# A two-layer hybrid model on one core: dense layer rows without their scale, and a last addition by column halves

## The chip, the cores and the metric

The kernel runs on one core of a Trainium2 chip. A time is that of one execution on the device in microseconds (us); what is shown for a kernel is the median of its runs. The core has TensorE (PE, with its weight loads apart as PEld), VectorE (DVE), ScalarE (ACT), GpSimd (POOL) and SyncE (SP, which here only starts transfers). They run side by side and wait for each other by semaphores: an instruction adds one to a semaphore when it is done, and another waits until the semaphore has reached a value.

## The reference

256 tokens of width 1024 go through two layers. The first is windowed attention and a dense gated layer, the second a gated delta rule and eight experts of which each token takes two. The stretches in which the change lies are the end of attention, the start of the dense layer, and the end of the experts:

```python
def rms_norm(x, w):
    y = x * rsqrt(mean(x * x, axis=-1, keepdims=True) + EPS)
    return y * w
def swiglu(h, w_gate, w_up, w_down):
    return (silu(h @ w_gate) * (h @ w_up)) @ w_down

h = h + swa_sink_attention(rms_norm(h, a_norm), ...)
h = h + swiglu(rms_norm(h, f_norm), f_w_gate, f_w_up, f_w_down)      # D_FF = 3584
h = h + gated_deltanet(rms_norm(h, b_norm), ...)
h = h + moe_swiglu(rms_norm(h, m_norm), ...)                          # 8 experts, top 2
return rms_norm(h, final_norm)
```

## The kernel before, in words

Tokens lie in two tiles of 128 rows (`t` = 0, 1) and 1024 columns; `h` holds the sum that runs through the layers. All products are in float32, made of three products each: the weights and the activations are split into a high part (ACT copies it, rounded) and a low part (DVE subtracts), and `mm3` (lines 342 to 345) adds high by high, low by high and high by low. Weights come from memory in pieces of 1 MB (`n`), through six raw buffers (`w_raw`), and are split into three buffers (`w_high`, `w_low`). `split_high` (line 331) waits until the piece has landed and until TensorE has used the piece three before it (`w_used`), and `split_low` (line 335) waits for `split_high`; SP starts the transfer of a piece when the piece six before it has been split (`lo_done`).

Every engine has one program, written out by hand; within it instructions run in the order in which they stand. So what the change does depends on which instruction stands where.

**From attention to the dense layer.** The output product of attention is made in pieces `out_piece(half, t, cb, bank)`; a piece is 12 products of 512 columns. The last four are those of `half` 1: t=0 with column blocks 0 and 1, then t=1 with 0 and 1. DVE adds each to `h` (`added`, line 2107). When a row tile of `h` is complete, ACT squares and sums it (`norm_tile`, line 693), POOL makes the reciprocal root (`norm`, lines 462 and 463: `rstd`), and DVE multiplies the rows by `rstd` and by the gain `f_gain` (`norm_tile`, line 2213: `xs`). TensorE turns these rows by eight transposes (`turn_tile`, line 1258), ACT and DVE make the high and the low part of the turned rows (lines 699 and 2115: `x_high`, `x_low`), and TensorE multiplies the first gate block with them (`first_gate(half, t)`, four pieces of 12 products). Then `up` and, in a loop over seven blocks of 512 columns, gate, up and down products follow. ACT applies silu (line 802), DVE multiplies the up product with it (`gated`, line 2286).

**The end of the experts.** Seven experts give their rows back through memory; POOL gathers them, and DVE adds them to `h` (line 2798). The rows of the eighth expert go back by products with a selection matrix (`last_back(b)`, lines 1974 and 1977, one for each half `b` of the 1024 columns; its result for t and b lies in bank 4 + 2t + b), and DVE adds them (`last_add(t, b)`, line 2745). Between the two stands the job loop, a loop over jobs 8 to 10 on each engine: it runs its body only where an expert has more than 128 tokens, and with these inputs there is no such job (the trace has 336 expert weight pieces, which are 8 experts of 42). Each engine reads the number of jobs into a register (`value_load`) and goes through the loop, three times over the body. Then ACT squares and sums the rows of `h` (line 676), POOL makes `rstd` (lines 462 and 463), DVE multiplies (`fin`, line 2843), and SP stores the four quarters.

Semaphore `added` counts the additions to `h` at the end; `last_ps` counts the last products.

Of the kernel before, what the change touches and what calls it, by code (L numbers as in the profile page):

```python
# [12 lines left out]
D = 1024  # L13
T = 256
TT = T // 128
KD = D // 128
F = 3584
CH = 512
# [67 lines left out]
def hybrid_kernel(nc, x, a_w_qkv, a_b_qkv, a_sinks, a_w_o, f_w_gate, f_w_up, f_w_down,  # L86
# [13 lines left out]
    with ExitStack() as ctx:  # L100
# [20 lines left out]
        col_w = sb("col_w", [128, NCOL])  # L121
        ss = sb("ss", [128, 5, TT])
        ms = sb("ms", [128, 5, TT])
        rstd = sb("rstd", [128, 5, TT])
# [321 lines left out]
        def _(pool):  # L446
# [181 lines left out]
            for st in ("att", "ffn", "gdn", "moe"):  # L628
# [19 lines left out]
                deltanet_pool()  # L648
            norm("fin")


        @block.scalar
        def _(act):
# [48 lines left out]
            def attention(n0):  # L702
# [22 lines left out]
                def probs_out(a):  # L725
                    t = ITEMS[a][1]
                    act.wait_ge(sem("probT_ps"), a + 1)
                    if a >= 2:
# [3 lines left out]
                        .then_inc(sem("probT_done"), 1)  # L732

                def o_high(half, t):
                    act.wait_ge(sem("tile_ps"), 2 * half + t + 1)
                    nc.scalar.activation(xH[:, 4 * half:4 * half + 4, 128 * t:128 * t + 128],
                                         PS[:, 0, :].rearrange("p (k c) -> p k c", k=4), ACT.Copy).then_inc(sem("tile_high"), 1)
# [51 lines left out]
                o_high(1, 1)  # L789
                norm_tile("ffn", 0)  # L790
                split_high(act, f0 + 1)
                turn_tile("ffn", 0)
                norm_tile("ffn", 1)
                split_high(act, f0 + 2)
                turn_tile("ffn", 1)
                split_high(act, f0 + 3)

            def ffn(n0):
                def silu(n, r):
                    act.wait_ge(w_used, n + r * RAW)  # L800
                    for t in range(TT):
                        nc.scalar.activation(fg[:, t], PS[:, t, :], ACT.Silu).then_inc(sem("f_silu_done"), 1)

                def turned(c):
                    for t in range(TT):
                        act.wait_ge(sem("f_turn_ps"), 2 * c + t + 1)
                        nc.scalar.activation(faH[:, t], PS[:, 6 + t, :].rearrange("p (f q) -> p f q", f=4), ACT.Copy)\
                            .then_inc(sem("f_high_done"), 1)

                silu(n0 + 2, 0)  # L810
                act.wait_ge(xs_done, TT * (norm_no["ffn"] + 1))
# [279 lines left out]
            def experts(n0):  # L1091
# [95 lines left out]
                with act.Fori(E, JOBS) as j:  # L1187
                    with act.If(j < njobs):
                        r0 = j * NC
                        turned_in(j)  # L1190
                        for n in range(4):
                            split_high(act, n0 + n, r0)
                        silu(n0 + 2, r0)
                        split_high(act, n0 + 4, r0)
                        split_high(act, n0 + 5, r0)
                        with act.Fori(0, NC - 1) as i:
                            step(r0 + i)
                        turned(r0 + NC - 1)
                        y_high(n0 + SUBS_FFN, r0)

            if "att" in stages:
# [5 lines left out]
            if "moe" in stages:  # L1207
                experts(base["moe"])
            norm("fin")


        @block.tensor
        def _(pe):
# [47 lines left out]
            def attention(n0):  # L1261
# [149 lines left out]
                out_piece(1, 0, 1, 3)  # L1411
                out_piece(1, 1, 0, 4)
                out_piece(1, 1, 1, 5)

            def ffn(n0):
# [11 lines left out]
                x0 = TT * norm_no["ffn"]  # L1427
                turn_tile("ffn", xs, 0, xs_done, x0 + 1)
                first_gate(0, 0)
                first_gate(1, 0)  # L1430
                turn_tile("ffn", xs, 1, xs_done, x0 + 2)
                first_gate(0, 1)
# [449 lines left out]
            def experts(n0):  # L1882
# [86 lines left out]
                def last_back(b):  # L1969
                    o = [PS[:, 4 + 2 * t + b, :] for t in range(TT)]  # L1970
                    c = slice(CH * b, CH * b + CH)
                    pe.wait_ge(sem("ys_high"), b + 1)
                    for t in range(TT):
# [5 lines left out]
                def back(j):  # L1979

                    pe.wait_ge(sem("ys_low"), j + 3)
                    for t in range(TT):
                        for b in range(2):
                            o = PS[:, 4 + 2 * t + b, :]
# [50 lines left out]
                pe.wait_ge(sem("m_act_done"), E * NC)  # L2035
                turned()
                pe.wait_ge(sem("m_low_done"), E * NC)
                last_down(n0 + 4, E * NC - 1)

                pe.wait_ge(sem("jobs_done"), 1)  # L2040
                njobs = pe.value_load(jobs[0:1, NJ:NJ + 1], min_val=E, max_val=JOBS)
                with pe.Fori(E, JOBS) as j:
                    with pe.If(j < njobs):
                        r0 = j * NC
                        pe.wait_ge(sem("ys_low"), 2)
                        pe.wait_ge(sem("added"), 4 * j)
                        turn_in(j)
# [11 lines left out]
                        back(j - E)  # L2059
                pe.wait_ge(sem("added"), njobs * 4)  # L2060
                last_back(0)
                last_back(1)

# [11 lines left out]
        def _(dve):  # L2075
# [42 lines left out]
            def attention(n0):  # L2118
# [162 lines left out]
            def ffn(n0):  # L2281
                def gated(c, n, r):
                    dve.wait_ge(w_used, n + r * RAW)
                    for t in range(TT):
                        dve.wait_ge(sem("f_silu_done"), 2 * c + t + 1)
                        V.tensor_tensor(fa[:, t], PS[:, 2 + t, :], fg[:, t], ALU.mult).then_inc(sem("f_act_done"), 1)

# [13 lines left out]

                dve.sem_inc(sem("f_y_free"), 1)
                gated(0, n0 + 4, 0)
                split_low(dve, n0 + 5)
# [16 lines left out]
            def deltanet(n0):  # L2321
                def last_gated(t):
                    return V.tensor_tensor(fa[:, t], PS[:, 2 + t, :], fg[:, t], ALU.mult)

# [306 lines left out]
            def experts(n0):  # L2631
# [92 lines left out]
                def add(c, e):  # L2724
                    dve.wait_ge(sem("back_ps"), c + 1)
                    dve.wait_ge(sem("added"), 4 * (LAST + 1) + 4 * c)
                    for t in range(TT):
                        for b in range(2):
                            col = slice(CH * b, CH * b + CH)
# [71 lines left out]
                last_y_low(0)  # L2801
                last_y_low(1)
                with dve.Fori(E, JOBS) as j:
                    with dve.If(j < njobs):
# [14 lines left out]
                        add(j - E, e)  # L2819
                dve.wait_ge(sem("added"), njobs * 4)  # L2820
                for t in range(TT):
                    for b in range(2):
# [60 lines left out]
```

## Time and profile before

| what | us |
|---|---|
| median of 3 runs | 1541.15 |
| lowest and highest run | 1535.83, 1541.67 |
| the profiled execution's own time | 1540.96 |
| its span | 1539.2 |
| PE busy | 1502.5 (98%) |
| DVE busy | 1211.9 (79%) |
| ACT busy | 974.6 (63%) |
| POOL busy | 148.8 (10%) |

The span is the time from the first to the last instruction that the profiler recorded; the execution's own time is 1.76 us longer. A row of the timeline gives start, duration, engine, line, operation, what is written and read, and in brackets how long the engine had been idle before, and which instruction ended that. A matmul of 512 columns is shown as 0.39 us, but the next one starts 0.23 us after it, since they are pipelined.

### The profile page before, as it was taken

To read this page: it belongs to the slowest core of one execution; us is meant where nothing else is said; L and a number is where in the kernel's file an instruction comes from. 1 tells how busy PE (TensorE), PEld (TensorE's weight loads), DVE (VectorE), ACT (ScalarE), POOL (GpSimd) and SP (SyncE) were. 2 spreads that over 40 slices of the span, in tenths; PEclk is the share of its full clock that TensorE was granted. 3 is DMA by queue.
4 is the path that set the end of the run, shared out by engine and by line. 5 is a ranking of instruction groups with operands and counts; after the bars stand their busy time and mean duration, and the time that the engine had idled before them with its cause. 6 is when DMAs were issued, how large, how long until landed. Compare 5 with 4: busy or idle time off the path is not lost.

```text
span 1539.2 us, 22172 instructions
## 1 busy us (share of the span) xinstructions
PE 1502.5 (98%) x8236; PEld 1260.7 (82%) x8236; DVE 1211.9 (79%) x947; ACT 974.6 (63%) x789; POOL 148.8 (10%) x159
## 2 busy tenths in 40 slices
PE   7999999999999999999999999999999999999996
PEld 6878888879997888888888888888888888888885
DVE  6764555556785568888888888888889888888987
ACT  5544333345555347777777777777777777777774
POOL 1021000001424109300000000000000000000100
PEclk9999999999999999999999999999999999999999
DMA  9349555555331228999999999999999999999992
GB/s 365 109 153 401 196 186 184 191 163 167 110 109 57 81 85 325 403 415 392 372 366 403 374 369 392 375 379 381 378 379 379 379 377 379 392 368 365 423 399 102
DMA packets 90971, 455.05 MB, mean 296 GB/s; under 512 B 7712, under 2 KB 8112, under 8 KB 47920
## 3 DMA queue, kind: packets, MB, share of 16 engines
q1 hardware_dynamic: 83984, 430.86, 73.7%
q0 software_dynamic: 6080, 22.29, 3.7%
q10 hardware_dynamic: 864, 1.29, 0.3%
q8 instruction: 32, 0.52, 0.1%
q14 instruction: 11, 0.09, 0.0%
HBM read 438.68 MB, written 15.73 MB: 295 GB/s over the span
## 4 chain that ended last, share of the span: by engine, by line
PE 92%; DVE 3%; ACT 2%; POOL 1%; issue 1%; DMA 0%; DVEq 0%; SPq 0%; POOLq 0%; ACTq 0%
PE PS L343 28%; PE PS L345 27%; PE PS L344 27%; PE PS L1576 2%; PE PS L1941 2%; PE PS L1330 1%; DVE w_low L335 1%; PE PS L1556 1%; PE PS L1304 0%; DMA w_raw<-in_a_w_qkv 0%; PE PS L1992 0%; ACT w_high L331 0%; PE PS L1319 0%; PE PS L1453 0%; DVE cv L2366 0%
## 5 line engine op out<-in xcount | busy, mean ns | idle before, releaser
L335 DVE TENSOR_TENSOR w_low<-w_raw,w_high 128x2048 fp32r<-128x2048 f32 x406 | 931.4, 2297 | 177.6 <-ACT w_high L331 176.8
L331 ACT ACTIVATE w_high<-w_raw 128x2048 fp32r<-128x2048 f32 x406 | 777.5, 1918 | 287.1 <-PE PS L345 282.1
L343 PE MATMUL PS<-w_high,x_high 128*128 128x512 f32 x1264 | 502.7, 398 | 5.2 <-DVE x_low L2115 2.1
L345 PE MATMUL PS<-w_high,x_low 128*128 128x512 f32 x1264 | 494.1, 391 | 0.0
L344 PE MATMUL PS<-w_low,x_high 128*128 128x512 f32 x1264 | 493.2, 390 | 0.0
L343 PEld LDWEIGHTS PS<-w_high,x_high 128*128 128x128 f32 x1264 | 238.2, 188 | 56.4 <-DVE w_low L335 4.0
L345 PEld LDWEIGHTS PS<-w_high,x_low 128*128 128x128 f32 x1264 | 237.7, 188 | 51.0
L344 PEld LDWEIGHTS PS<-w_low,x_high 128*128 128x128 f32 x1264 | 238.3, 189 | 46.9
L343 PE MATMUL PS<-w_high,m_act_high 128*128 128x512 f32 x448 | 175.1, 391 | 1.6 <-DVE m_act_low L2760 1.6
L344 PE MATMUL PS<-w_low,m_act_high 128*128 128x512 f32 x448 | 174.4, 389 | 0.0
L345 PE MATMUL PS<-w_high,m_act_low 128*128 128x512 f32 x448 | 174.4, 389 | 0.0
L343 PEld LDWEIGHTS PS<-w_high,m_act_high 128*128 128x128 f32 x448 | 84.1, 188 | 19.0 <-DVE m_act_low L2760 1.8
L345 PEld LDWEIGHTS PS<-w_high,m_act_low 128*128 128x128 f32 x448 | 84.1, 188 | 17.5
L344 PEld LDWEIGHTS PS<-w_low,m_act_high 128*128 128x128 f32 x448 | 84.1, 188 | 17.3
L1137 ACT ACTIVATE m_act_high<-PS 128x512 fp32r<-128x512 f32 x56 | 33.5, 599 | 70.1 <-PE PS L1941 70.1
L343 PE MATMUL PS<-x_high,w_high 128*128 128x256 f32 x192 | 56.1, 292 | 0.0
L344 PE MATMUL PS<-x_low,w_high 128*128 128x256 f32 x192 | 54.3, 283 | 0.0
L345 PE MATMUL PS<-x_high,w_low 128*128 128x256 f32 x192 | 54.3, 283 | 0.0
L524 POOL DMA_DIRECT2D x_slots<-x_slots_dram x6 | 3.2, 534 | 502.5 <-PE PS L1992 502.5
L2756 DVE TENSOR_TENSOR m_act<-PS,m_gate 128x512 f32<-128x512 f32 x56 | 38.3, 684 | 1.2 <-PE PS L345 1.2
L2760 DVE TENSOR_TENSOR m_act_low<-PS,m_act_high 128x512 fp32r<-128x512 f32 x56 | 38.2, 683 | 0.0
L343 PE MATMUL PS<-w_high,f_act_high 128*128 128x512 f32 x96 | 37.6, 391 | 0.0
(324 smaller groups left out, 1231.3 us busy)
## 6 DMA issues: line engine op xcount, KB each, us to landing
w_raw<-in_m_w_blocks SPq DMA_DIRECT2D x336, 1024.0 KB, 7.1
w_raw<-in_b_w_in SPq DMA_DIRECT2D x16, 1024.0 KB, 5.4
w_raw<-in_f_w_gate SPq DMA_DIRECT2D x14, 1024.0 KB, 5.0
w_raw<-in_f_w_up SPq DMA_DIRECT2D x14, 1024.0 KB, 5.1
w_raw<-in_f_w_down SPq DMA_DIRECT2D x14, 1024.0 KB, 4.8
x_slots_dram<-zeros POOLq DMA_DIRECT2D x12, 512.0 KB, 8.2
w_raw<-in_a_w_qkv SPq DMA_DIRECT2D x5, 1024.0 KB, 17.3
w_raw<-in_a_w_o SPq DMA_DIRECT2D x4, 1024.0 KB, 15.4
```

Of the source, the lines that this page charges most:

```text
L331: nc.scalar.activation(WH[:, n % SPLIT, :], W[:, n % RAW, :], ACT.Copy).then_inc(hi_done, 1)
L335: nc.vector.tensor_tensor(WL[:, n % SPLIT, :], W[:, n % RAW, :], WH[:, n % SPLIT, :].bitcast(f32), ALU.subtract).then_inc(lo_done, 1)
L343: nc.tensor.matmul(o, sH, mH, start=first, stop=False)
L344: nc.tensor.matmul(o, sH, mL, start=False, stop=False)
L345: return nc.tensor.matmul(o, sL, mH, start=False, stop=last)
L1137: nc.scalar.activation(maH[:], PS[:, 4, :].rearrange("p (f q) -> p f q", f=4), ACT.Copy)\
L1330: last = nc.tensor.matmul(PS[:, 1, (AD + 1) * hh:(AD + 1) * (hh + 1)], probT[:, a % 2, hh * (t + 1) + kt, :], vals[:, kt, g, :], start=(kt ...
L1556: last = nc.tensor.matmul(PS[:, bank + hg, 128 * (hh % 4):128 * (hh % 4) + 128], lhs(hh), rhs(hh), start=True, stop=True)
L1576: last = nc.tensor.matmul(PS[halves(s), INV + s, HALF * hh:HALF * hh + HALF], lhs(s, hh), rhs(s, hh), start=True, stop=True)
L1941: last = nc.tensor.transpose(PS[:, 4, 128 * f:128 * f + 128], ma[:, 128 * f:128 * f + 128], ident)
L2756: V.tensor_tensor(ma[:], PS[:, 1, :], mg[:], ALU.mult).then_inc(sem("m_act_done"), 1)
L2760: V.tensor_tensor(maL[:], PS[:, 4, :].rearrange("p (f q) -> p f q", f=4), maH[:].bitcast(f32), ALU.subtract).then_inc(sem("m_low_done"), 1)
```

## The change

Two parts. In the dense layer the rows go to TensorE as `h` times the gain, without `rstd`; the scale is applied behind the products instead, inside silu (`scale=rstd`) and inside the multiplication with the up product. The order of the instructions at the entry of the dense layer changes with it on DVE, ACT and TensorE, and the squares are written to `prob` instead of `xs`. At the end, TensorE's `last_back` and DVE's `last_add` come ahead of the job loop, additions go by column halves, ACT squares each half of 512 columns after the job loop, and POOL adds the two half sums in the `tensor_scalar` that it has anyway. TensorE reads the number of jobs ahead of its last down products.

```diff
+            n = norm_no["fin"]
+            for t in range(TT):
+                s = slice(t, t + 1)
+                pool.wait_ge(ss_done, TT * n + t + 1)
+                link(nc.gpsimd.tensor_scalar(ss_half[:, 0, s], ss_half[:, 0, s], 1.0 / D, EPS, ALU.mult, ALU.add))
+            for t in range(TT):
+                s = slice(t, t + 1)
+                pool.wait_ge(ss_done, TT * n + TT + t + 1)
+                link(nc.gpsimd.tensor_scalar(ms[:, n, s], ss_half[:, 1, s], 1.0 / D, ss_half[:, 0, s], ALU.mult, ALU.add))
+                nc.gpsimd.tensor_tensor(rstd[:, n, s], ms[:, n, s], neg_half[:, s], ALU.pow).then_inc(rstd_done, 1)
...
+                def dense_square(t):
+                    n = norm_no["ffn"]
+                    act.wait_ge(h_done, TT * (n - 1) + t + 1)
+                    nc.scalar.activation(prob[:, t], h[:, t].rearrange("p (n k) -> p n k", n=AG), ACT.Square, accum_out=ss[:, n, t:t + 1]).then_inc(ss_done, 1)
...
-                norm_tile("ffn", 0)
+                turn_tile("ffn", 0)
                 split_high(act, f0 + 1)
-                turn_tile("ffn", 0)
-                norm_tile("ffn", 1)
+                dense_square(0)
+                turn_tile("ffn", 1)
                 split_high(act, f0 + 2)
-                turn_tile("ffn", 1)
+                dense_square(1)
                 split_high(act, f0 + 3)
...
-                        nc.scalar.activation(fg[:, t], PS[:, t, :], ACT.Silu).then_inc(sem("f_silu_done"), 1)
+                        nc.scalar.activation(fg[:, t], PS[:, t, :], ACT.Silu, scale=rstd[:, norm_no["ffn"], t:t + 1]).then_inc(sem("f_silu_done"), 1)
...
+                for b in range(2):
+                    c = slice(CH * b, CH * b + CH)
+                    for t in range(TT):
+                        act.wait_ge(sem("added"), njobs * 4 + (TT * b + t + 1))
+                        nc.scalar.activation(xs[:, t, c], h[:, t, c], ACT.Square, accum_out=ss_half[:, b, t:t + 1]).then_inc(ss_done, 1)
...
                 out_piece(1, 1, 0, 4)
+                turn_tile("ffn", xs, 0, xs_done, TT * norm_no["ffn"] + 1)
                 out_piece(1, 1, 1, 5)
...
-                turn_tile("ffn", xs, 0, xs_done, x0 + 1)
                 first_gate(0, 0)
+                turn_tile("ffn", xs, 1, xs_done, x0 + 2)
                 first_gate(1, 0)
-                turn_tile("ffn", xs, 1, xs_done, x0 + 2)
...
                 turned()
+                pe.wait_ge(sem("jobs_done"), 1)
+                njobs = pe.value_load(jobs[0:1, NJ:NJ + 1], min_val=E, max_val=JOBS)
                 pe.wait_ge(sem("m_low_done"), E * NC)
                 last_down(n0 + 4, E * NC - 1)
-
-                pe.wait_ge(sem("jobs_done"), 1)
-                njobs = pe.value_load(jobs[0:1, NJ:NJ + 1], min_val=E, max_val=JOBS)
+                last_back(0)
+                last_back(1)
                 with pe.Fori(E, JOBS) as j:
...
-                pe.wait_ge(sem("added"), njobs * 4)
-                last_back(0)
-                last_back(1)
...
-                    dve.wait_ge(rstd_done, TT * n + t + 1)
-                    dve.wait_ge(h_done, t + 1)
-                    V.scalar_tensor_tensor(out=xs[:, t], in0=h[:, t], scalar=rstd[:, n, t:t + 1], in1=f_gain[:],
-                                           op0=ALU.mult, op1=ALU.mult).then_inc(xs_done, 1)
+                    dve.wait_ge(h_done, TT * (n - 1) + t + 1)
+                    V.tensor_tensor(xs[:, t], h[:, t], f_gain[:], ALU.mult).then_inc(xs_done, 1)
...
+                norm_tile(0)
                 added(1, 1, 0)
-                norm_tile(0)
+                turn_tile("ffn", 0)
                 added(1, 1, 1)
-                turn_tile("ffn", 0)
+                norm_tile(1)
                 split_low(dve, f0 + 1)
-                norm_tile(1)
                 turn_tile("ffn", 1)
...
-                        V.tensor_tensor(fa[:, t], PS[:, 2 + t, :], fg[:, t], ALU.mult).then_inc(sem("f_act_done"), 1)
+                        V.scalar_tensor_tensor(out=fa[:, t], in0=PS[:, 2 + t, :], scalar=rstd[:, norm_no["ffn"], t:t + 1], in1=fg[:, t],
+                                               op0=ALU.mult, op1=ALU.mult).then_inc(sem("f_act_done"), 1)
...
+                dve.wait_ge(sem("added"), 4 * E)
+                for b in range(2):
+                    for t in range(TT):
+                        dve.wait_ge(sem("last_ps"), 2 * b + t + 2)
+                        last_add(t, b).then_inc(sem("added"), 1)
                 with dve.Fori(E, JOBS) as j:
...
-                dve.wait_ge(sem("added"), njobs * 4)
-                for t in range(TT):
-                    for b in range(2):
-                        dve.wait_ge(sem("last_ps"), 2 * b + t + 2)
-                        last = last_add(t, b)
-                    last.then_inc(h_done, 1)
```

How the instructions stand. On TensorE, at the entry of the dense layer, before; `x_high` is the turned row tile, `xs` the rows that are turned, and each row with a wait is the first of 12 products, of which the others are left out:

```order
L343 MATMUL PS<-w_high,x_high 128x512 [waits tile_low,lo_done]
...
L1258 MATMUL PS<-cst,xs 128x128 [waits xs_done]
L1258 MATMUL PS<-cst,xs 128x128 x7
L343 MATMUL PS<-w_high,x_high 128x512 [waits tile_low,lo_done]
...
L343 MATMUL PS<-w_high,x_high 128x512 [waits tile_low,lo_done]
...
L1258 MATMUL PS<-cst,xs 128x128 [waits xs_done]
L1258 MATMUL PS<-cst,xs 128x128 x7
L343 MATMUL PS<-w_high,x_high 128x512 [waits tile_low,lo_done]
```

and in the changed program, from the output piece ahead of the last one (line 1278 is the transposes' line there):

```order
L344 MATMUL PS<-w_high,x_high 128x512 [waits tile_low,lo_done]
...
L1278 MATMUL PS<-cst,xs 128x128 [waits xs_done]
L1278 MATMUL PS<-cst,xs 128x128 x7
L344 MATMUL PS<-w_high,x_high 128x512 [waits tile_low,lo_done]
...
L344 MATMUL PS<-w_high,x_high 128x512 [waits tile_low,lo_done]
...
L1278 MATMUL PS<-cst,xs 128x128 [waits xs_done]
L1278 MATMUL PS<-cst,xs 128x128 x7
L344 MATMUL PS<-w_high,x_high 128x512 [waits tile_low,lo_done]
```

Before, tile 0 is turned behind the last output piece and tile 1 behind both gate pieces of tile 0; now tile 0 is turned ahead of the last output piece and tile 1 between the two gate pieces of tile 0.

On DVE at the same place, before (line 2107 adds to `h`, 2213 scales the rows, 2115 is the low part of the turned rows, 335 that of the weights):

```order
L2107 TENSOR_TENSOR h<-PS,h 128x512 [waits piece_ps]
L2107 TENSOR_TENSOR h<-PS,h 128x512 [waits w_used]
L2213 SCALAR_TENSOR_TENSOR xs<-h,rstd,f_gain 128x1024 [waits h_done,rstd_done,loaded_att]
L2107 TENSOR_TENSOR h<-PS,h 128x512 [waits w_used]
L2115 TENSOR_TENSOR x_low<-PS,x_high 128x4x128 [waits tile_high] x2
L335 TENSOR_TENSOR w_low<-w_raw,w_high 128x2048 [waits hi_done]
L2213 SCALAR_TENSOR_TENSOR xs<-h,rstd,f_gain 128x1024 [waits h_done,rstd_done,loaded_att]
L2115 TENSOR_TENSOR x_low<-PS,x_high 128x4x128 [waits tile_high] x2
```

and now:

```order
L2125 TENSOR_TENSOR h<-PS,h 128x512 [waits piece_ps]
L2230 TENSOR_TENSOR xs<-h,f_gain 128x1024 [waits h_done,loaded_att]
L2125 TENSOR_TENSOR h<-PS,h 128x512 [waits w_used]
L2133 TENSOR_TENSOR x_low<-PS,x_high 128x4x128 [waits tile_high] x2
L2125 TENSOR_TENSOR h<-PS,h 128x512 [waits w_used]
L2230 TENSOR_TENSOR xs<-h,f_gain 128x1024 [waits h_done,loaded_att]
L336 TENSOR_TENSOR w_low<-w_raw,w_high 128x2048 [waits hi_done]
L2133 TENSOR_TENSOR x_low<-PS,x_high 128x4x128 [waits tile_high] x2
```

The rows of tile 1 (`xs`) now stand ahead of the low part of the weight piece, and both stand behind the last addition to `h`.

On TensorE at the end, before, from the last of the down products to the loop, and then from the loop's end:

```order
L345 MATMUL PS<-w_high,m_act_low 128x512
L2041 TENSOR_LOAD jobs [waits jobs_done]
L2041 ISA x2
L2042 UNCONDITIONAL_BRANCH
L2043 COMPARE_AND_BRANCH
...
L2042 COMPARE_AND_BRANCH
L2060 REGISTER_ALU
L1974 MATMUL PS<-y_last_high,pick_last 128x512 [waits ys_high,added]
```

and now:

```order
L346 MATMUL PS<-w_high,m_act_low 128x512
L1995 MATMUL PS<-y_last_high,pick_last 128x512 [waits ys_high,added]
L1995 MATMUL PS<-y_last_high,pick_last 128x512
L1998 MATMUL PS<-y_last_low,pick_last 128x512 [waits ys_low]
L1998 MATMUL PS<-y_last_low,pick_last 128x512
L1995 MATMUL PS<-y_last_high,pick_last 128x512 [waits ys_high,added]
L1995 MATMUL PS<-y_last_high,pick_last 128x512
L1998 MATMUL PS<-y_last_low,pick_last 128x512 [waits ys_low]
L1998 MATMUL PS<-y_last_low,pick_last 128x512
L2064 UNCONDITIONAL_BRANCH
```

The register load and the loop no longer stand between the last down product and the products that bring the rows back. The loop's body is 262 rows on TensorE; on DVE it is 55 and on ACT 41, and there it now stands between the additions and `fin`, and still ahead of the squares.

## Rows read from the trace of the kernel before

**Rows 1.** The page, part 1.
```profile
PE 1502.5 (98%) x8236; PEld 1260.7 (82%) x8236; DVE 1211.9 (79%) x947; ACT 974.6 (63%) x789; POOL 148.8 (10%) x159
```

**Rows 2.** Waits of PE: total us, times, longest.
```profile
PE PS L1974 <- issue: 2.4, 1, 2.4
PE PS L343 <- DVE x_low L2115: 2.1, 2, 1.1
```

**Rows 3.** PE's timeline, dense entry: start, duration, engine, line, what, idle before.
```profile
99.42 0.39 PE L343 MATMUL PS<-w_high,x_high 128*128 128x512 f32 x1
...
104.25 0.47 PE L343 MATMUL PS<-w_high,x_high 128*128 128x512 f32 x1 [1.07 <-DVE x_low L2115]
...
109.84 1.04 PE L1258 MATMUL PS<-cst,xs 128*128 128x128 f32 x8
111.94 0.47 PE L343 MATMUL PS<-w_high,x_high 128*128 128x512 f32 x1 [1.06 <-DVE x_low L2115]
...
117.47 0.39 PE L343 MATMUL PS<-w_high,x_high 128*128 128x512 f32 x1
```

**Rows 4.** PE's timeline, dense loop: eight transposes with no wait behind them.
```profile
139.24 1.03 PE L1453 MATMUL PS<-cst,f_act 128*128 128x128 f32 x8
140.03 0.48 PE L343 MATMUL PS<-w_high,x_high 128*128 128x512 f32 x1
```

**Rows 5.** DVE's timeline, dense entry.
```profile
100.23 1.27 DVE L2213 SCALAR_TENSOR_TENSOR xs<-h,rstd,f_gain 128x1024 f32<-128x1024 f32 x1
102.34 0.69 DVE L2107 TENSOR_TENSOR h<-PS,h 128x512 f32<-128x512 f32 x1 [0.84 <-PE PS L345]
...
104.61 2.28 DVE L335 TENSOR_TENSOR w_low<-w_raw,w_high 128x2048 fp32r<-128x2048 f32 x1
```

**Rows 6.** ACT's timeline, dense entry.
```profile
99.68 1.92 ACT L331 ACTIVATE w_high<-w_raw 128x2048 fp32r<-128x2048 f32 x1 [0.90 <-PE PS L345]
```

**Rows 7.** DVE's groups in the dense layer: count, busy us, mean ns, idle before.
```profile
L2286 DVE TENSOR_TENSOR f_act<-PS,f_gate 128x512 f32<-128x512 f32 x12 | 7.7, 682 | 5.1 <-PE PS L345 5.1
```

**Rows 8.** Stretches of the dense layer and of the experts: PE, PEld, DVE, ACT, POOL.
```profile
128.00:340.00 212.00, 212.00 (x965) 176.00 (x964) 117.64 (x88) 85.80 (x66) 2.95 (x6) 1.00 0.62 213
1000.00:1200.00 200.00, 200.00 (x912) 165.27 (x911) 177.40 (x99) 149.33 (x101) 2.14 (x4) 1.00 0.98 381
```

**Rows 9.** DMA issues: count, KB each, median us to landing.
```profile
w_raw<-in_m_w_blocks SPq DMA_DIRECT2D x336, 1024.0 KB, 7.1
```

**Rows 10.** PE's timeline, end.
```profile
1520.44 0.50 PE L343 MATMUL PS<-w_high,m_act_high 128*128 128x512 f32 x1 [1.59 <-DVE m_act_low L2760]
...
1525.79 0.39 PE L345 MATMUL PS<-w_high,m_act_low 128*128 128x512 f32 x1
1528.58 0.70 PE L1974 MATMUL PS<-y_last_high,pick_last 128*128 128x512 f32 x2 [2.40 <-issue]
```

**Rows 11.** DVE's timeline, end.
```profile
1526.85 0.69 DVE L2741 TENSOR_TENSOR y_last_low<-PS,y_last_high 128x512 fp32r<-128x512 f32 x1 [0.67 <-ACT y_last_high L1146]
1529.62 2.92 DVE L2745 SCALAR_TENSOR_TENSOR h<-PS,cw,h 128x512 f32<-128x512 f32 x4 [2.08 <-PE PS L1977]
1533.48 1.41 DVE L2843 SCALAR_TENSOR_TENSOR fin<-h,rstd,w_fin 128x512 f32<-128x512 f32 x2 [0.94 <-POOL rstd L463]
1535.34 1.41 DVE L2843 SCALAR_TENSOR_TENSOR fin<-h,rstd,w_fin 128x512 f32<-128x512 f32 x2 [0.45 <-POOL rstd L463]
```

**Rows 12.** The chain that ended last: start, us, what.
```profile
1530.47 2.08 DVE h L2745 x3
```

**Rows 13.** ACT's timeline, end.
```profile
1526.22 0.60 ACT L1146 ACTIVATE y_last_high<-PS 128x512 fp32r<-128x512 f32 x1 [0.76 <-PE PS L345]
...
1532.57 1.06 ACT L676 ACTIVATE xs<-h 128x1024 f32<-128x1024 f32 x1 [0.17 <-DVE h L2745]
```

**Rows 14.** POOL's timeline, end.
```profile
1532.50 0.19 POOL L462 TENSOR_SCALAR ms<-ss 128x1 f32<-128x1 f32 x1 [95.03 <-ACT xs L676]
...
1533.81 0.48 POOL L462 TENSOR_SCALAR ms<-ss 128x1 f32<-128x1 f32 x1 [0.46 <-ACT xs L676]
```

More of the change, by code:

```diff
@@ L122, in hybrid_kernel @@
         ss = sb("ss", [128, 5, TT])
+        ss_half = sb("ss_half", [128, 2, TT])
         ms = sb("ms", [128, 5, TT])
@@ L648, in _ @@
                 deltanet_pool()
-            norm("fin")
+            n = norm_no["fin"]
[8 more added lines that the diff above has]
+                nc.gpsimd.tensor_tensor(rstd[:, n, s], ms[:, n, s], neg_half[:, s], ALU.pow).then_inc(rstd_done, 1)
         @block.scalar
@@ L808, in turned @@
                             .then_inc(sem("f_high_done"), 1)
+                act.wait_ge(rstd_done, TT * (norm_no["ffn"] + 1))
                 silu(n0 + 2, 0)
@@ L1208, in _ @@
                 experts(base["moe"])
-            norm("fin")
         @block.tensor
@@ L1971, in last_back @@
                     c = slice(CH * b, CH * b + CH)
+                    pe.wait_ge(sem("added"), 1)
                     pe.wait_ge(sem("ys_high"), b + 1)
@@ L2044, in experts @@
                         r0 = j * NC
-                        pe.wait_ge(sem("ys_low"), 2)
-                        pe.wait_ge(sem("added"), 4 * j)
+                        pe.wait_ge(sem("added"), 4 * j + 4)
                         turn_in(j)
@@ L2302, in ffn @@
                 dve.sem_inc(sem("f_y_free"), 1)
+                dve.wait_ge(rstd_done, TT * (norm_no["ffn"] + 1))
                 gated(0, n0 + 4, 0)
@@ L2322, in last_gated @@
                 def last_gated(t):
-                    return V.tensor_tensor(fa[:, t], PS[:, 2 + t, :], fg[:, t], ALU.mult)
+                    return V.scalar_tensor_tensor(out=fa[:, t], in0=PS[:, 2 + t, :], scalar=rstd[:, norm_no["ffn"], t:t + 1], in1=fg[:, t],
+                                                  op0=ALU.mult, op1=ALU.mult)
                 def last_low_turned(t):
@@ L2725, in add @@
                     dve.wait_ge(sem("back_ps"), c + 1)
-                    dve.wait_ge(sem("added"), 4 * (LAST + 1) + 4 * c)
-                    for t in range(TT):
-                        for b in range(2):
+                    dve.wait_ge(sem("added"), 4 * (E + 1) + 4 * c)
+                    for b in range(2):
+                        for t in range(TT):
                             col = slice(CH * b, CH * b + CH)
@@ L2802, in experts @@
                 last_y_low(1)
+                dve.wait_ge(sem("added"), 4 * E)
+                for b in range(2):
+                    for t in range(TT):
+                        dve.wait_ge(sem("last_ps"), 2 * b + t + 2)
+                        last_add(t, b).then_inc(sem("added"), 1)
                 with dve.Fori(E, JOBS) as j:
@@ L2819, in experts @@
                         add(j - E, e)
-                dve.wait_ge(sem("added"), njobs * 4)
-                for t in range(TT):
-                    for b in range(2):
-                        dve.wait_ge(sem("last_ps"), 2 * b + t + 2)
-                        last = last_add(t, b)
-                    last.then_inc(h_done, 1)
             if "att" in stages:
```

## The prediction

> **What bounds the kernel now.** I read the page first. TensorE is busy for 98% of the span and no other engine for more than 79% [rows 1], so what counts is where TensorE waits, and the chain behind its last product. The waits of TensorE come second. Apart from the start of the program, where it waits for the first weights, the two longest groups are 2.4 us of "issue" ahead of the products of line 1974, and twice 1.1 us for `x_low` of line 2115 [rows 2]. The change works at exactly these two places. Third, the timelines of the two stretches, for the sum. Fourth, the rest: in the dense loop and in the experts TensorE is busy for the whole of its stretch [rows 8], so a microsecond won at the entry of the dense layer should arrive at the end, as long as the weights keep up.
>
> **Part 1, the entry of the dense layer.** Before, TensorE starts the last output piece at 99.42 and the first `up` product at 117.47 [rows 3]: 18.05 us for five pieces and two turns of a tile. Each turn costs eight transposes and a wait until the turned rows are split; from the transposes' start at 109.84 to the next product at 111.94 it is 2.10 us. Where TensorE doesn't wait behind eight transposes, they take 0.79 us (139.24 to 140.03 [rows 4]), and the next product 0.08 us more than the others.
>
> The new path, from the same 99.42: the rows of tile 0 are made as soon as `h` of tile 0 is complete, some 1.3 us [rows 5] (its last piece is issued one piece, 2.72 us, ahead of 99.42, and its addition starts some 0.4 us after that and takes 0.7: 97.6), so they are there at 98.9 and the transposes start at once, to 100.21. The last output piece takes 12 steps of 0.227 us and 0.08: TensorE issues its last product at 102.79 and is free at 103.0. The first gate piece needs `x_low` of tile 0, which was finished under the output piece, and ends at 105.75. Its cover is 2.8 us of output piece over some 1.9 us of splitting. Then the transposes of tile 1, to 106.6.
>
> Now what is late next. The piece behind them, gate with the second half of the columns, needs the low part of the second weight piece. On DVE this stands behind the last addition to `h` and behind the rows of tile 1. The addition starts 0.43 us after the last product was issued (before, 102.34 after 101.91 [rows 5]), so at 103.22, and takes 0.69; the rows take 1.28; the low part 2.28: DVE is done at 107.45. ACT has the high part earlier: it may start it at 99.68 [rows 6], and now starts it behind the turned rows at about 101.1, to 103.0. So TensorE waits from 106.6 to 107.5, a new wait of 0.9 us. From there three pieces run without a stop (36 steps of 0.2267 us and 0.08), and `up` starts at 115.7. The gain is 117.47 - 115.7 = **1.75 us**. Two waits of 1.07 and 1.06 plus 0.24 us of transposes that are seen to take less go; 0.9 comes. The bounds: 2.6 if the low part were in time, and 0.3 if the new wait took 2.3 us, which it would if ACT's high part came 1.4 us after DVE is free for the low one.
>
> What is added in the loop costs nothing on TensorE. The 14 `gated` instructions take 0.68 us each [rows 7] and get a scalar; the addition at the end, which has one, takes 0.73 (2.92 for four [rows 11]). That is 14 times 0.05, 0.7 us on DVE, which stands idle for 94 of the 212 us of the dense loop [rows 8]. If TensorE were waiting for them it would be 0.7 us in all. `rstd` now has until silu of the first block. The squares of tile 1 stand behind the turned rows (107.5) and one weight piece (1.9) and end about 110.6, POOL's two instructions need some 1.5 us (1533.81 to 1535.34 at the end), and silu can't start ahead of 116.
>
> **Part 2, the end.** TensorE issues the last down product at 1525.79, and the first product back at 1528.58, after 2.40 us of "issue" [rows 10]: nothing that it waits for comes after 1527.5, it is loading the register and going three times around the job loop. Now the load stands ahead of the last down products, where TensorE waits for 1.59 us anyway [rows 10]. It would cost something only if it took longer than that, and since load and loop together take 2.4 us, that is 0.8 us at the worst.
>
> So the products of column half 0 start at 1526.0 and are done at 1527.0. Half 1 needs its low part from DVE, 1526.85 + 0.69 = 1527.54 [rows 11], and is done at 1528.2. DVE's four additions start right behind that low part, at 1527.57, one each 0.69 us (2.08 for three [rows 12]), and the third needs half 1 at 1528.95, long done. The last one ends at 1527.57 + 3 x 0.69 + 0.74 = 1530.4. Before, it is 1529.62 + 2.92 = 1532.54. **-2.15 us.**
>
> Behind it: ACT's square of 1024 columns takes 1.06 us, started at 1532.57 [rows 13], and POOL follows at 1533.81 [rows 14]. A copy of 2048 takes 1.92 [rows 6], so 512 columns less are worth 0.43 us, and for the second row tile POOL starts 0.8 us after the last addition, at 1531.25. But `fin` of the two tiles is 2 x 1.41 us on DVE [rows 11]. For tile 0 the addition ends at 1529.7, POOL starts at 1530.5, and from POOL's start to `fin` it is 0.98 us (1532.50 to 1533.48 [rows 11, 14]): 1531.5. For tile 1 POOL's two instructions need 1.53 us (1533.81 to 1535.34): 1532.8, and DVE isn't free before 1532.9. So `fin` ends at 1534.3, against 1536.75 before: a gain of 2.45 us at best.
>
> What takes some of it back is the job loop. ACT dispatches its last copy at 1526.22 [rows 13] and has to be through the loop by 1528.3 for the first square. DVE goes through it behind the last addition, which it can dispatch from 1529.0 or 1529.7 on, and has to be through by 1531.5. No row shows the loop alone. From below it costs nothing, if DVE's sequencer runs ahead of its additions; from above it is TensorE's 2.4 us from 1529.7 on, so 1532.1, which delays `fin` by 0.6. I take 0.3 from the middle. For ACT, 2.4 us from 1526.22 is 1528.6, and it makes up for this, since a half square (0.63) is shorter than an addition. Then the four stores follow as before. Part 2 gives **2.1 us**, between 1.1 and 2.5.
>
> The Trainium skill, Runtime: NRT & Kernel Launch, section Instruction fetch mechanics, says that a taken branch to outside the two 16 KiB pages that an engine holds has to fetch code first. By that rule TensorE's 2.4 us are the price of a body of 262 rows, the bodies on DVE (55) and ACT (41) are short enough to be held, the loop costs less there, and the end would gain its full 2.45. No row here shows a loop on DVE by itself, so the sum stays with the middle.
>
> **The sum.** 1.75 + 2.1 = 3.85 us. The profiled execution took 1540.96 us for itself (span 1539.2); with the change 1537.1, span 1535.35. The median of the runs is 0.2 above that execution, so **1537.3 us**, 0.25% less. A measurement of this kernel can't tell less than about 0.5%, 7.7 us, from no change: its own three runs lie between 1535.83 and 1541.67.
>
> **The rivals.**
> - The end gives little. The job loop costs DVE and ACT more than TensorE, and only starts when the last instruction ahead of it is done: DVE is ready for `fin` at 1530.4 + 2.4 = 1532.8, ACT's squares start at 1529.2, `fin` ends at 1535.6, a gain of 1.1. For it: the registers and branches are the same on all engines. Against: instructions follow each other without a gap elsewhere, so sequencers run ahead. Time 1541.15 - 1.75 - 1.1 = 1538.3.
> - The dense entry gives little. The new wait for the low part is 2.3 us and not 0.9, because ACT's high part of the second weight piece comes late behind the turned rows. For it: the change moves both the weight's parts behind other work. Against: ACT has 2 us to spare. Time 1541.15 - 0.3 - 2.1 = 1538.75.
> - The run falls in the lower of the two levels that the three runs show, 1535.83 against 1541.4. I know no cause for it in the trace. Against: two of three, and the profiled execution, are in the upper. Time 1541.15 - 3.85 - 5.3 = 1532.0.
> - Slower. The experts' stage is at the edge of the transfers: their engines are busy for 98% of it at 381 GB/s [rows 8], and a piece of 1 MB must come each 12 x 0.2267 = 2.72 us, which is 385 GB/s. If starting earlier shifted the weights against POOL's stores and gathers so that TensorE had to wait, each of the 336 pieces would cost its share: 0.018 us each is 6 us, more than the whole gain, and the time 1543.3. It decides from the point where a piece takes as long to land as its buffer gives it, six pieces (16.3 us) less the two splits of 2.3 and 1.9, so 12 us. Against: the median is 7.1 us [rows 9], and TensorE never waits in the stage.
>
> **How the numbers follow.** The forecast 0.62, the end gives little 0.09, the dense entry gives little 0.09, the lower level 0.16, slower 0.04. The range 1531.5 to 1541 takes in the forecast, both small cases and the lower level with the bounds of the unknown costs; above it lies the slower case. The likeliest case by itself is 1536.3 to 1538.5. Faster by over 0.5% means under 1533.4, which is the lower level alone, most of it: 0.15. Slower by over 0.5% means above 1548.9, a part of the slower case: 0.02. The rest, 0.83, is within 0.5%.
>
> **What would show it.** Right: TensorE's waits for `x_low` at the dense entry are gone and one of about 0.9 us for `w_low` (line 336) stands ahead of the gate piece; 16.3 us from the start of the last output piece's transposes to `up`; the 2.40 us of "issue" are gone, and TensorE doesn't wait longer than 1.6 us ahead of the last down products; the first addition of column half 0 starts within 0.1 us of the low part; from the last addition to the span's end 6.3 to 6.7 us (before 6.66). Wrong: a wait in front of TensorE in the experts' stage; idle time by "issue" ahead of `fin` or of the squares, which is the job loop; a `w_low` wait over 2 us; or a wait for `f_act` in the dense loop.

## The result: slower by 0.3%, and the profile after

| what | before | changed |
|---|---|---|
| median | 1539.05 us (15 runs) | 1544.48 us (15 runs) |
| lowest, highest run | 1535.61, 1541.67 | 1541.3, 1548.03 |
| ratio | | 1.0034, interval 1.0024 to 1.0045 |
| span of the profiled execution | 1539.2 | 1544.6 |

Both parts of the change do what they were forecast to do, and the kernel is slower by 5.4 us all the same. The page of the changed kernel shows TensorE at the same share and with the same number of products as before [rows 1], and 9.4 us busier:

```profile
PE 1511.9 (98%) x8236; PEld 1261.2 (82%) x8236; DVE 1212.8 (79%) x947; ACT 976.3 (63%) x793; POOL 149.9 (10%) x161
```

First the two places of the change. In the waits of TensorE (total, times, longest), the 2.4 us of "issue" and the two waits for `x_low` of line 2115 [rows 2] are gone. The largest that stand behind the program's start:

```profile
PE PS L344 <- DVE w_low L336: 2.1, 3, 1.1
PE PS L344 <- DVE m_act_low L2779: 1.5, 1, 1.5
```

TensorE's timeline at the entry of the dense layer, to be held against [rows 3]: `up` starts at 115.86, where it started at 117.47 before, and the new wait for `w_low` is 0.72 us.

```profile
99.41 1.03 PE L1278 MATMUL PS<-cst,xs 128*128 128x128 f32 x8
...
105.77 1.03 PE L1278 MATMUL PS<-cst,xs 128*128 128x128 f32 x8
107.52 0.50 PE L344 MATMUL PS<-w_high,x_high 128*128 128x512 f32 x1 [0.72 <-DVE w_low L336]
...
115.86 0.39 PE L344 MATMUL PS<-w_high,x_high 128*128 128x512 f32 x1
```

DVE's timeline there [rows 5]: the rows of tile 1 hold up the low part of the weights, which ends at 107.47.

```profile
97.68 1.23 DVE L2230 TENSOR_TENSOR xs<-h,f_gain 128x1024 f32<-128x1024 f32 x1
...
104.04 1.23 DVE L2230 TENSOR_TENSOR xs<-h,f_gain 128x1024 f32<-128x1024 f32 x1
105.18 2.29 DVE L336 TENSOR_TENSOR w_low<-w_raw,w_high 128x2048 fp32r<-128x2048 f32 x1
```

The end, TensorE's timeline [rows 10]: the first product back follows the last down product after 0.23 us.

```profile
1528.19 0.50 PE L344 MATMUL PS<-w_high,m_act_high 128*128 128x512 f32 x1 [1.50 <-DVE m_act_low L2779]
...
1533.65 0.39 PE L346 MATMUL PS<-w_high,m_act_low 128*128 128x512 f32 x1
1533.88 0.61 PE L1995 MATMUL PS<-y_last_high,pick_last 128*128 128x512 f32 x2
```

DVE's timeline at the end [rows 11]. The additions are done 4.39 us after the last down product was issued (6.75 before), and the four `fin` instructions stand in one piece:

```profile
1535.32 2.72 DVE L2764 SCALAR_TENSOR_TENSOR h<-PS,cw,h 128x512 f32<-128x512 f32 x4
1539.37 2.74 DVE L2861 SCALAR_TENSOR_TENSOR fin<-h,rstd,w_fin 128x512 f32<-128x512 f32 x4 [1.33 <-POOL rstd L659]
```

ACT's squares at the end [rows 13] begin right behind the first addition (1535.32 + 0.69) and keep its pace, so the job loop did not hold them up:

```profile
1536.09 0.63 ACT L1220 ACTIVATE xs<-h 128x512 f32<-128x512 f32 x1 [1.42 <-DVE h L2764]
```

From the last down product to the end of the span it is 1544.62 - 1533.65 = 10.97 us, against 1539.2 - 1525.79 = 13.41 before: 2.4 us gained.

Now the place where nothing was changed. The stretches of the dense loop and of the experts, same columns as [rows 8]:

```profile
128.00:340.00 212.00, 212.00 (x956) 174.31 (x955) 117.39 (x87) 85.37 (x66) 6.07 (x11) 1.00 0.63 216
1000.00:1200.00 200.00, 200.00 (x906) 164.16 (x906) 176.38 (x99) 148.25 (x101) 2.14 (x4) 1.00 0.98 377
```

TensorE is busy for the whole of both, as before, at the full granted clock, but it makes 956 products where it made 965, and 906 where it made 912. No wait shows it: the products start further apart in time. The 24 down products in the timeline above go from 1528.19 to 1533.65, 5.46 us from the first start to the last; before, from 1520.44 to 1525.79, 5.35 us [rows 10]. The table is taken from the starts of all products in both traces, by kind, as means over 37 steps of the experts and 5 of the dense loop (a step is one block of 512 hidden columns, with its gate, up and down products):

| start to start, ns | before | changed |
|---|---|---|
| up products (experts) | 227.2 | 227.2 |
| gate products (experts) | 226.7 | 226.7 |
| down products (experts) | 226.7 | 233.2 |
| down products (dense) | 226.7 | 233.4 |
| one step of the experts, us | 16.81 | 16.96 |
| one step of the dense loop, us | 33.55 | 33.87 |

TensorE's start times at four places, and the end of the span, give the account: at the first turn of `f_act` the changed kernel is 1.6 us ahead (137.62 against 139.24), at the dense layer's last product 0.5 behind (341.79 against 341.27), at the experts' first turn still 0.6 behind, at the last down product 7.9 behind, and at the end 5.4. So it is 1.6 us gained, 2.1 lost in the dense layer, 7.3 lost in the experts and 2.4 gained, in all 5.4 lost.

### The profile page after: what moved, and what is told of

It reads as the page before. It is cut to its first block, busy times and chain, and to the rows that moved or that the text cites. A ratio compares the mean times of both kernels' runs of the same rounds, so it can differ in the third digit from the quotient of the medians.

```text
span 1544.6 us, 22184 instructions
## 1 busy us (share of the span) xinstructions
PE 1511.9 (98%) x8236; PEld 1261.2 (82%) x8236; DVE 1212.8 (79%) x947; ACT 976.3 (63%) x793; POOL 149.9 (10%) x161
## 4 chain that ended last, share of the span: by engine, by line
PE 93%; DVE 3%; POOL 1%; ACT 1%; issue 1%; DMA 0%; DVEq 0%; SPq 0%; POOLq 0%
PE PS L344 28%; PE PS L346 28%; PE PS L345 28%; PE PS L1596 2%; PE PS L1961 2%; PE PS L1350 1%; DVE w_low L336 1%; PE PS L1576 1%; PE PS L1324 0%; PE PS L2013 0%; PE PS L1339 0%; DMA h<-in_x 0%; PE PS L1473 0%; DVE cv L2385 0%; POOL ssq L550 0%
## 6 DMA issues: line engine op xcount, KB each, us to landing
w_raw<-in_a_w_qkv SPq DMA_DIRECT2D x5, 1024.0 KB, 14.1
```

## The experiments

In a product one tile is stationary (128 columns of it are loaded first, a row of PEld) and the other is moving (512 columns of it, the row of PE). The stationary side of the down products is `f_act_high` and `f_act_low`, or `m_act_high` and `m_act_low`; that of gate and up is `x_high` and `x_low`. The moving side is `w_high` and `w_low` in all of them. The new tile `ss_half` is allocated behind `ss` and ahead of the stage tiles. It holds 16 bytes of numbers in each partition, and by the program's addresses it takes up 32: `m_act_high` lies at 174112 instead of 174080, and `f_act_high` at 153632 instead of 153600, while `w_high` (2048) and `x_high` (116736) stay. That this move slows the products was the first theory (A); its rival (B) was that the new order of the engines' work does, their phase against each other.

Four of the runs below have a ratio with an interval. It is against the kernel before in runs made beside them, whose median was 1540.65 us over 21 runs; the plain quotient of the medians differs from it by up to 0.001.

**The tiles back in their places.** The changed kernel with this edit:

```diff
-        sb("pad_stages", [128, 496])
+        sb("pad_stages", [128, 488])
```

Expected: 

> The changed kernel with one edit: the padding ahead of the stage tiles is 32 bytes shorter, which takes back the 32 bytes that the new tile ss_half put in front of them, so that f_act_high, m_act_high and all other stage tiles lie where they lay before. Order and number of instructions as in the changed kernel. Theory A (the place of the tiles): the down products of both stages go back from 0.232 us each to 0.227, one expert step from 16.96 to 16.80 us, one dense step from 33.87 to 33.53; what is left is the gain of both parts, 1.65 + 2.4 = 4.1 us, so ratio 0.9974 and about 1535.0 us. Theory B (the new order of the engines, their phase against each other, slows the down products): nothing changes, 16.96 us a step and about 1544.5.

Measured: 1535.91 us (5 runs), ratio 0.9961, interval 0.9947 to 0.9974. Down products 226.7 ns, steps of 16.81 and 33.55 us. Its stretch of the experts:

```profile
1000.00:1200.00 200.00, 200.00 (x914) 165.26 (x913) 177.70 (x99) 148.07 (x100) 2.15 (x4) 1.00 0.98 382
```

Theory A stands and B falls: no instruction differs from the changed kernel. This version is faster than the changed kernel and than the kernel before.

**The kernel before, moved.** The kernel before with one line more, a tile that nothing uses:

```diff
         ss = sb("ss", [128, 5, TT])
+        ss_half = sb("ss_half", [128, 2, TT])
```

Expected: 

> The kernel before with one edit: the tile ss_half is allocated and never used, which moves all stage tiles by 32 bytes. Not one instruction differs. Theory A: down products 0.232 us each, expert step 16.96 us, dense step 33.87; the time is what the changed kernel lost against its gain, 5.4 + 4.1 = 9.5 us more, about 1548.5, ratio 1.006. Theory B: same as before, 1539.05, ratio 1.000.

Measured: 1549.29 us (5 runs), ratio 1.0048, interval 1.0035 to 1.0062. Down products 233.2 and 233.4 ns, steps 16.97 and 33.87 us. The stretch has the 906 products of the changed kernel:

```profile
1000.00:1200.00 200.00, 200.00 (x906) 164.13 (x905) 176.38 (x99) 147.97 (x100) 2.14 (x4) 1.00 0.98 378
```

From the experts' first turn to the last down product TensorE takes 941.5 us, against 941.4 in the changed kernel and 934.1 in the kernel before. So the loss comes without any of the change's instructions.

**Each part alone**, all stage tiles in their old places. The diff is the change's own, cut in two; the end part has `ss_half` and, to make up for it, `pad_stages` with 488 columns. Expected of the dense part: 

> Only the dense layer's part of the change, no ss_half, all tiles in their old places. Theory A: the two waits of 1.07 us give way to one of 0.7 us for w_low, up starts 1.65 us earlier, nothing gives it back: 1537.4, ratio 0.9989; expert step 16.80. Theory B: if this part's order slows the down products, expert step 16.96 and about 1547.

Expected of the end part: 

> Only the part of the change at the end of the experts, with ss_half and 32 bytes less padding, so that the stage tiles keep their places. Theory A: expert step 16.80 us, from the last down product to the span's end 10.9 us instead of 13.4: 1536.6, ratio 0.9984. Theory B: if this part slows the experts, step 16.96 and about 1544.

Measured: the dense part 1538.03 us (11 runs), ratio 0.9978 (0.9968 to 0.9989); the end part 1538.86 us (11 runs), ratio 0.9984 (0.9973 to 0.9996). The steps are 16.81 and 33.55 us in both runs. The two ratios multiply to 0.9962, close to the 0.9961 of both together. In microseconds that is 5.9, more than the 4.0 that the traces of the kernel before and of the changed kernel give (1.6 + 2.4), though the interval (0.9947 to 0.9974) reaches down to 4.0. In its trace the dense part has a wait of 0.71 us for `w_low` where the two for `x_low` were; the end part has 11.1 us from the last down product to the end. The end of the profiled execution of the dense part is 1.7 us longer than that of before, at the wait that it still has (TensorE's timeline):

```profile
1524.42 1.19 PE L1980 MATMUL PS<-y_last_high,pick_last 128*128 128x512 f32 x2 [2.74 <-issue]
```

The stretch around it, same columns as [rows 8]:

```profile
1521.00:1528.00 7.00, 4.08 (x12) 2.64 (x10) 2.50 (x5) 0.60 (x1) 0.00 (x0) 0.76 0.01 2
```

Its mean granted clock is 0.76: for 3.4 us, from 1523.87 on, the lower level of 1.2 GHz was granted, which began while TensorE stood still for 2.74 us, and two products take 1.19 us instead of 0.70. It doesn't come from this part of the change. The run with all tiles moved by 32 bytes (below) has the very instructions of the kernel before, which kept the full clock there, and shows the same:

```profile
1525.76 1.19 PE L1974 MATMUL PS<-y_last_high,pick_last 128*128 128x512 f32 x2 [2.54 <-issue]
```

Of the ten traces here that have this wait by "issue" (2.1 to 2.7 us), four got the lower level for some of the products behind it, and they take 14.1 to 15.1 us from the last down product to the end of the span; the other six take 13.2 to 13.6. The three traces without the wait take 11.0 to 11.1. So the end part gains 2.4 us against one execution and up to 4.1 against another. That is an explanation of the larger gain in the ratios, not shown run by run.

**Which tile.** Three runs of the kernel before, each with another tile moved. Only the experts' tiles:

```diff
+            sb("pad_act", [128, 8], c=c)
             maH = sb("m_act_high", [128, 4, 128], f32r, c=c)
```

Expected: 

> The kernel before with 32 bytes of padding in front of m_act_high, so that m_act_high, m_act_low and the experts' tiles behind them move by 32 bytes, and nothing of the dense layer. Theory A1 (the stationary tile of the down products, m_act_high and m_act_low, is what must lie right): expert down products 0.233 us each, step 16.97; dense down products stay at 0.2267. Theory A2 (another of the tiles that moved, such as m_gate, m_act, xs_high or ys_high, disturbs): expert step stays at 16.81.

Only `w_high` and `w_low`, 32 bytes lower (they are the moving side of gate, up and down products alike):

```diff
-        sb("pad_weights", [128, 224])
+        sb("pad_weights", [128, 216])
...
+        sb("pad_raw", [128, 8])
         W = sb("w_raw", [128, RAW, SUB])
```

Expected: 

> The kernel before with w_high and w_low, the moving side of the down products and the stationary side of none but the gates' (there it is the moving side too), 32 bytes lower, all other tiles in their places. If only a stationary tile's place counts: all products stay at 0.2267 us. If the moving tile's place counts, or the place of the two tiles to each other: gate, up and down products all at 0.233, expert step about 17.27, the dense step about 34.5.

Only `x_high` and `x_low` (with `pad_stages` at 488):

```diff
+        sb("pad_x", [128, 8])
         xH = sb("x_high", [128, KD, T], f32r)
```

Expected: 

> The kernel before with x_high and x_low (stationary in gate and up products) 32 bytes higher, the stage tiles in their places (ss, ms, rstd and neg_half, which are small, move too). Theory A1, the stationary tile's place: gate and up products 0.233 us each and down products 0.2267, expert step 16.80 + 48 x 0.0065 = 17.12, dense step about 34.2. Otherwise nothing changes.

Measured, one run each: with the experts' tiles moved, 1548.84 us; down products of the experts 233.2 ns, those of the dense loop 226.7. With the weights moved, 1571.22 us, all products 233.2 to 233.3 ns, 17.23 us a step. With the x tiles moved, 1557.25 us, gate and up 233.1 to 233.3 ns and down 226.7. The stretch of the experts with the weights moved:

```profile
1000.00:1200.00 200.00, 200.00 (x892) 161.68 (x891) 173.85 (x98) 145.90 (x98) 1.60 (x3) 1.00 0.98 370
```

The same stretch with the x tiles moved:

```profile
1000.00:1200.00 200.00, 200.00 (x900) 162.81 (x899) 174.36 (x97) 147.40 (x100) 2.15 (x4) 1.00 0.97 373
```

So moving either side slows the products that use it, and only those. That the stationary tile alone counts, as one theory had it, is wrong.

**How far, and from what.** The kernel before again, with other widths of the same paddings. The diff is abridged: four runs in one block, and in the last two `pad_stages` is narrower by the width of `pad_x` (464 and 240 columns), so that the stage tiles stay.

```diff
# stage tiles by 64 bytes
+        sb("pad_stages", [128, 512])
# everything by 32 bytes
+        sb("pad_weights", [128, 232])
# x, f_act, m_act tiles by 128, 256, 512 bytes
+        sb("pad_x", [128, 32]); sb("pad_f", [128, 64]); sb("pad_act", [128, 128])
# x, f_act, m_act tiles by 1024, 512, 1024 bytes
+        sb("pad_x", [128, 256]); sb("pad_f", [128, 128]); sb("pad_act", [128, 256])
```

Expected of 64 bytes: 

> The kernel before with all stage tiles moved by 64 bytes instead of 32. If a tile has to start at a multiple of 64 bytes: down products 0.2267, expert step 16.81, the time of before. If it has to start at a larger multiple (the tiles m_act_high and f_act_high lay at multiples of 2048): 0.233 and 16.97 as with 32 bytes, or another value between.

Expected of 128, 256 and 512: 

> The kernel before with three different moves, each of the stationary tiles of one kind of product: x_high and x_low by 128 bytes (gate and up of both stages), f_act_high and f_act_low by 256 (dense down), m_act_high and m_act_low by 512 (experts' down). They lay at multiples of 2048 bytes. Each kind of product shows by itself whether such a distance is enough for 0.2267 us or leaves it at 0.233. If 128 bytes are enough, all are 0.2267 and the expert step is 16.81; if only multiples of 2048 do, all are 0.233, the expert step 17.23.

Expected of 1024 and 512: 

> The kernel before with x_high and x_low 1024 bytes higher, f_act_high and f_act_low 512, m_act_high and m_act_low 1024. With the run of 128, 256 and 512 bytes this gives the smallest distance at which a product is back at 0.2267 us; the dense down products repeat the 512 bytes of the experts' down products there.

Expected of all by 32: 

> The kernel before with 32 bytes more padding in front of everything: the weights, the x tiles and the stage tiles all move by 32 bytes together. If it is the distance of the stationary and the moving tile to each other that counts, all products stay at 0.2267 us and the time is that of before. If each tile's own start counts: 0.233 or slower in all, expert step 17.23 or more, time at least 1570.

Measured, one run each: 1551.47, 1556.40, 1541.13 and 1539.60 us. By kind of product:

| stationary tile moved against the weights by | ns, start to start |
|---|---|
| 0 (before) | 226.7 |
| 32 bytes | 233.2 |
| 64 | 233.3 |
| 128 | 232.4 (x tiles) |
| 256 | 226.7 (dense down) |
| 512 | 226.7 (dense down), 227.4 (experts' down) |
| 1024 | 226.7 |
| both moved by 32 | 226.7 |

The 227.4 is a mean: of a step's 24 down products the last 16 follow each other by 226.7 as well, and the ones ahead of them, which come behind the slow products of the x tiles, by up to 231.

The last line of the table decides what counts. With everything 32 bytes higher, no tile of the products starts where it started, and the experts' stretch is as fast as before:

```profile
1000.00:1200.00 200.00, 200.00 (x914) 165.28 (x913) 177.74 (x99) 148.07 (x101) 2.14 (x4) 1.00 0.99 382
```

It is the distance of the two tiles to each other, and of the distances tried all multiples of 256 bytes are fast (0, 256, 512, 1024) and the three others slow (32, 64, 128); none between 128 and 256 was tried, and 256 itself only in the dense down products. A theory of each tile's own start had forecast at least 1570 us. What in the chip does this stays open: the traces show products that start further apart, no wait, and weight loads as long as before (188 ns in both).

## Why the prediction was wrong

- **The dense entry: right.** Forecast 1.75 us with a new wait of 0.9 for `w_low`; measured 1.6 us (117.47 to 115.86) with a wait of 0.72. DVE was done at 107.47, where the working had 107.45. The sentence that names the terms has a slip: the 0.24 us of transposes goes at each of the two turns, so 2.13 + 0.5 - 0.9 = 1.73; with one of them it would be 1.5.
- **The end: right, a little low.** Forecast 2.1 us; measured 2.4. The register load ahead of the last down products cost nothing (that wait is 1.50 us, 1.59 before), the additions gained 2.36 us against 2.15, and the job loop, for which I had subtracted 0.3, cost nothing: `fin` waits 1.33 us for POOL behind the last addition, in DVE's timeline above, and no idle time by "issue" stands there. How long the loop takes on DVE doesn't show, only that it is hidden behind that wait. The 2.44 us are the 2.45 of the case in which the loop costs nothing.
- **The step that failed** is the one that says "what is added in the loop costs nothing on TensorE", so that the sum has two gains and no loss. It counted instructions: the multiplications went from 682 to 744 ns, about as said (730), and stayed hidden. It left out the one line that adds no instruction, the allocation of `ss_half`. It cost 9.4 us, 2.1 + 7.3 by TensorE's start times, where the sum had nothing: 336 dense and 1344 expert down products by some 6.6 ns would give 11. In the experts a part of this is taken up elsewhere: the seven steps with a change of expert take 17.83 to 17.87 us before and 17.83 to 17.84 now, as long as ever.
- **"A microsecond won at the entry should arrive at the end"** held, as the run with the tiles in their places shows. But the ground for it was too weak. TensorE "busy for the whole of its stretch" [rows 8] says that it doesn't wait, not that it keeps its rate; the number of products in the same row says that. And none of the four signs that the prediction gives for being wrong appeared: it looked for waits, and a slower rate is none.
- **The rivals.** The slower case had the right place (the experts), by luck nearly the right size (6 us, 7.3 measured) and the wrong cause: no wait for weights stands in that stretch. The transfers move 377 GB/s instead of 381, which fits a TensorE that uses up the pieces more slowly. No case in the list had a slower TensorE. The end didn't give little (2.4 us, not 1.1), and neither did the dense entry (a wait of 0.72 us, not 2.3). The rival of a lower level of the runs is taken up below.
- **The range** ended at 1541 and left out every unknown that isn't an instruction. The starting value was high too: the median of the three runs before was 1541.15, that of 15 is 1539.05.

## What to carry to other kernels

A new tile moves every tile behind it. Where TensorE is the bound, compare the addresses of its stationary and moving tiles before and after: here the distances of 32, 64 and 128 bytes over a multiple of 2048 cost 3% of each product, and those of 256, 512 and 1024 nothing. And where an engine is busy all the time before and after, count its instructions in equal stretches of both traces; a slower rate shows in no wait.

## What the runs showed of the hardware that I had not expected

The place of two tiles to each other sets the pace of float32 products of 512 columns: 226.7 ns at the multiples of 256 bytes that were tried, 232.4 to 233.3 at 32, 64 and 128 bytes.

The levels of the runs, too, have a visible part. The kernel before and the end part alone have the same instructions around 570 us of their spans, the end part 1.6 us ahead. First the kernel before:

```profile
560.00:576.00 16.00, 14.96 (x84) 13.02 (x83) 9.41 (x25) 4.43 (x5) 0.98 (x1) 0.89 0.19 67
```

The end part alone:

```profile
560.00:576.00 16.00, 16.00 (x103) 14.29 (x102) 10.33 (x26) 6.20 (x9) 3.57 (x9) 1.00 0.23 75
```

In the first, the lower level of the clock was granted for 3.4 us from 568.5 on, 7 us after a wait of 1.04 us that ended at 561.3; in the second it was not granted, though the same wait is there, and the stretch from the last product of the delta rule's output to the first turn in the experts took 36.5 us against 34.9. Near 505 us the lower level lasted 6.8 us in one and 3.4 in the other, another 1.2 us. That is 2.8 us, and the products at the end, at one level or the other, make up to 1.6 more (15.0 against 13.4 us from the last down product to the end, with the same instructions). The lowest and the highest run of the kernel before are 6 us apart; what the rest is stays open, and so does what sets the level in an execution.
